# Strassen's scheme for half of the input projections of a differential attention layer (one core, fp32r)

## The reference, cut to what matters

```python
proj = u @ w_in                                   # (512, 2048) @ (2048, 8192)
q, k = split_heads(proj[..., :E], 16), split_heads(proj[..., E:2*E], 16)
v, z = split_heads(proj[..., 2*E:3*E], 8), proj[..., 3*E:4*E]
logits = q_blk @ k.T * scale + rel_bias           # masked above the diagonal
p = softmax(logits).reshape(B, 8, 2, Q_BLOCK, S)
a = p[:, :, 0] - lam * p[:, :, 1]
o = rms_norm(a @ v, subln_g) * (1.0 - lam_init)
y = (merge_blocks(o) * silu(z)) @ w_out           # (512, 2048) @ (2048, 2048)
h = layer_norm(ALPHA * x + y, ln_g, ln_b)
```

## Time and profile before

| | |
|---|---|
| median of 3 runs | 942.35 us |
| the profiled execution: its own time, its span | 942.39 us, 940.6 us |
| TensorE busy | 99% of the span, granted clock 1.00 |
| VectorE, ScalarE, GpSimd busy | 59%, 34%, 7% |
| HBM traffic | 121 GB/s over the span |
| one pair (1 to 7) | 94.2 us, 384 projection matmuls |

### The profile page before, as it was taken

The page is one execution under the profiler, slowest core; times in us unless marked ns, Lnnn a source line. Parts: engine busy times, 40 slices in busy tenths (PEclk is TensorE's granted clock), DMA queues, the critical chain, the costliest instruction groups (busy, mean ns, idle before and its releaser), DMA issues.

```text
span 940.6 us, 11611 instructions
## 1 busy us (share of the span) xinstructions
PE 934.3 (99%) x4202; PEld 777.6 (83%) x4202; DVE 550.5 (59%) x1131; ACT 318.1 (34%) x558; POOL 66.4 (7%) x140
## 2 busy tenths in 40 slices
PE   9999999999999999999999999999999999999997
PEld 8888888888888888888888888888888888888886
DVE  5546764766466646664666466646664797324466
ACT  4423333333333333333333333333333454122311
POOL 2200010001000100010001000100000000000033
PEclk9999999999999999999999999999999999999999
DMA  8732342223222322232224222422232223542423
GB/s 317 270 104 72 100 132 97 82 95 134 93 85 94 135 92 86 94 135 91 87 92 137 90 88 89 139 89 89 90 112 89 89 90 122 201 159 90 157 103 121
DMA packets 34087, 108.88 MB, mean 116 GB/s; under 512 B 4352, under 2 KB 6400, under 8 KB 33808
## 3 DMA queue, kind: packets, MB, share of 16 engines
q1 hardware_dynamic: 28320, 93.60, 29.5%
q0 software_dynamic: 2336, 9.48, 3.0%
q10 hardware_dynamic: 3408, 5.51, 1.7%
HBM read 104.34 MB, written 9.48 MB: 121 GB/s over the span
## 4 chain that ended last, share of the span: by engine, by line
PE 99%; DMA 0%; DVE 0%; issue 0%; ACT 0%; SPq 0%; DVEq 0%; ACTq 0%
PE proj L1003 79%; PE att L1003 20%; DMA w_raw<-w_in_tiles_dram 0%; DVE big L995 0%; DVE last_stats L981 0%; ACT bias L654 0%; SPq L322 0%; DVE w_split L851 0%; DVE mean_var L984 0%; DVEq L983 0%; ACTq L653 0%
## 5 line engine op out<-in xcount | busy, mean ns | idle before, releaser
L1003 PE MATMUL proj<-w_split,xg_split 128*128 128x512 f32 x1680 | 385.2, 389 | 0.0
L1003 PEld LDWEIGHTS proj<-w_split,xg_split 128*128 128x128 f32 x1680 | 314.8, 188 | 65.2
L1003 PE MATMUL proj<-xg_split,w_split 128*128 128x512 f32 x1536 | 353.0, 389 | 0.2 <-DVE w_split L851 0.2
L1003 PEld LDWEIGHTS proj<-xg_split,w_split 128*128 128x128 f32 x1536 | 287.5, 188 | 59.6 <-issue 0.5
L460 ACT ACTIVATE w_split<-w_raw 128x1024 fp32r<-128x1024 f32 x128 | 135.8, 1061 | 383.6 <-PE proj L1003 354.5
L675 DVE TENSOR_TENSOR w_split<-w_raw,w_split 128x1024 fp32r<-128x1024 f32 x128 | 155.5, 1224 | 175.6 <-ACT w_split L460 173.8
L749 DVE STREAM_TRANSPOSE scratch<-scratch 32x192 f32<-32x192 f32 (+2 forms) x384 | 141.8, 369 | 5.2
L1003 PE MATMUL att<-w_split,xg_split 128*128 128x512 f32 x432 | 99.9, 389 | 0.0
L1003 PEld LDWEIGHTS att<-w_split,xg_split 128*128 128x128 f32 x432 | 81.0, 188 | 16.8
L928 DVE TENSOR_TENSOR w_split<-w_raw,w_split 128x1024 fp32r<-128x1024 f32 x25 | 30.5, 1225 | 58.1 <-ACT w_split L619 58.0
L421 POOL TENSOR_SCALAR mean_sq<-sq_sum 128x1 f32<-128x1 f32 x32 | 10.3, 323 | 701.6 <-ACT scratch L511 700.3
(11 more groups left out here) (116 smaller groups left out, 428.1 us busy)
## 6 DMA issues: line engine op xcount, KB each, us to landing
w_raw<-w_in_tiles_dram SPq DMA_DIRECT2D x126, 512.0 KB, 3.3
w_raw<-w_out_tiles_dram SPq DMA_DIRECT2D x32, 512.0 KB, 3.3
bias_by_distance<-bias_lines POOLq DMA_DIRECT2D x8, 640.0 KB, 5.1
bias<-bias_by_distance POOLq DMA_DIRECT2D x8, 512.0 KB, 4.1
x_res<-in_x_dram ACTq DMA_DIRECT2D x4, 1024.0 KB, 6.2
big<-x_cols_dram SPq DMA_DIRECT2D x7, 512.0 KB, 9.1
out_dram<-big SPq DMA_DIRECT2D x10, 256.0 KB, 2.5
w_raw<-w_in_tiles_dram SPq DMA_DIRECT2D x4, 256.0 KB, 4.7
```

The source lines that it names most:

```text
L1003: return nc.tensor.matmul(dst, lhsT, rhs, start=start, stop=stop, skip_group_check=True)
```

## The change

For pairs 1 to 7, the first eight k-tiles of the q/k product and those of the v/z product are done by Strassen's scheme (in a form with few additions) on a 2 x 2 block split: seven block products of half size in place of eight. x is cut into k-tiles 0 to 3 and 4 to 7, and positions 0 to 255 and 256 to 511; the weights into the same k-tiles and two column blocks. The last eight k-tiles are multiplied as before. A pair now has 22 slots (`SLOTS`), two phases of 11 (`PHASE`): seven block products, then four plain quarters. Phase h = 0 is q and k, h = 1 is v and z. A block product has 24 matmuls of **256** moving columns.

- **x sums** (`x_sum`, `x_sum_lo`, `x_sum_hi`): four block sums of x, made and split once, during pair 0, into `x_sums`, which lies where `big` (raw x, later the output rows and `g`) was.
- **weight sums** (`w_sum`): four per phase on VectorE, each a TENSOR_TENSOR of 128x1024; the sums then go through the same splits as the raw blocks. There are 22 splits a pair in place of 16.
- **PSUM bookkeeping**: after product 1 ScalarE copies a result (`keep_copies`) and VectorE adds another to it (`keep_sums`); after product 3 ScalarE copies the corners (`keep_corners`) and VectorE adds both back into PSUM (`seed_corners`); then `seed_highs` writes the last regions. TensorE waits for `sum_kept` ahead of product 4, for `corner_seeded` ahead of product 5, for `high_seeded` ahead of product 6.
- **g goes through DRAM**: since `x_sums` holds `big`'s place, ScalarE stores each pair's gated output (`g_stored`, a DMA on its queue), and SP reloads seven of them in pair 7, once slot 17 is done. VectorE's first `combine` of a pair waits for `g_stored`.
- **order**: scores t = 0, 1 now come after slot 16 and t = 2, 3 after slot 18 of 22, `weigh_v` after slots 6 and 8, `turn_gated` in slot 10, ahead of `k_chunk`, `turn_a_early` in slot 20. All three transposes stay on VectorE and keep their number and size.

```diff
-                for j in range(QUARTERS):
-                    if j < VZ:
-                        quarter(p, j)
+                for j in range(SLOTS):
+                    if j % PHASE < 7:
+                        product(p, j)
+                    elif j < PHASE:
+                        plain_qk(p, j)
                     else:
-                        vz_part(p, j)
-                    late_inserts(p - 1, j)
-                    own_inserts(p, j)
+                        plain_vz(p, j)
+                    inserts(p, j)
...
+            def product(p, j):
+                h, r = j // PHASE, j % PHASE
+                pe.wait_ge(w_ready, slots_before(p) + j + 1)
...
+                for group in range(2):
+                    if opens and h == 0:
+                        bank = 2 * group + side
+                        pe.wait_ge(vz_moved, p * ST - ST + bank + 1)
...
+                    elif opens:
+                        pe.wait_ge(k_moved, 2 * p + group + 1)
+                    elif r == 4:
+                        pe.wait_ge(sum_kept, phases_before(p) + h + 1)
+                    elif r == 5:
+                        pe.wait_ge(corner_seeded, 2 * (phases_before(p) + h) + group + 1)
+                    elif r == 6:
+                        pe.wait_ge(high_seeded, 2 * (phases_before(p) + h) + group + 1)
...
+                    for kk in range(SK):
+                        first = opens and kk == 0
+                        if h == 0:
+                            mm(dst, w[0][:, kk, part], xs[0][:, kk], first, False)
+                            mm(dst, w[0][:, kk, part], xs[1][:, kk], False, False)
+                            last = mm(dst, w[1][:, kk, part], xs[0][:, kk], False, False)
...
+            def w_sum(p, h, n):
+                b11, b12, b22, b21 = (w_raw[:, i] for i in range(4))
+                if n == 1:
...
+                    op = nc.vector.tensor_tensor(b12, b12, b11, ALU.subtract)
+                elif n == 2:
...
+                    op = nc.vector.tensor_tensor(raw_fifth, b22, b12, ALU.subtract)
+                elif n == 3:
+                    op = nc.vector.tensor_tensor(b11, raw_fifth, b11, ALU.subtract)
+                else:
+                    op = nc.vector.tensor_tensor(raw_fifth, b21, raw_fifth, ALU.subtract)
+                op.then_inc(t_ready, 1)
...
+            def slot(p, j):
+                h, r = j // PHASE, j % PHASE
+                if j == PHASE:
                     k_chunk(p)
+                if 17 <= j < 20:
+                    logits_of(p, j - 17)
+                if j == 20:
                     combine(p, 2)
                     logits_of(p, 3)
                 split_lo_at(p, j)
+                if r == 0:
+                    w_sum(p, h, 4)
+                if r == 2:
+                    keep_sums(p, h)
+                if r == 3:
+                    seed_corners(p, h)
+                if r == 4:
+                    seed_highs(p, h)
+                late_steps(p - 1, j)
...
+                    if r == 8:
+                        w_sum(ahead, half, 1)
+                        w_sum(ahead, half, 2)
+                    if r == 9:
+                        w_sum(ahead, half, 3)
+                if j == 9:
                     q_chunk(p)
+                if j == 21:
+                    combine(p, 3)
+                if j == 20:
                     turn_a_early(p)
```

More of the change, by code:

```diff
@@ L417, in _ @@
                     spread_bias(p + 1)
+            load_bias(0)
+            for p in range(PAIRS):
+                if p + 1 < PAIRS:
+                    load_bias(p + 1)
                 for t in range(ST):
@@ new lines, in seed_corners @@
+            def seed_corners(p, h):
+                for group in range(2):
+                    n = 2 * (phases_before(p) + h) + group + 1
+                    dve.wait_ge(copy_kept, 3 * (phases_before(p) + h) + group + 2)
+                    low, corner = region(h, group, 1, 0), region(h, group, 1, 1)
+                    nc.vector.tensor_tensor(low, low, kept_sum[:, group], ALU.add).then_inc(low_seeded, 1)
+                    dve.wait_ge(low_seeded, n)
+                    nc.vector.tensor_tensor(corner, low, kept_copy[:, group], ALU.add).then_inc(corner_seeded, 1)
@@ L739, in combine @@
                 dve.wait_ge(mix_ready, n)
+                if t == 0 and not first_pair(p):
+                    dve.wait_ge(g_stored, 16 * p)
                 cols = slice(0, (t + 1) * P)
@@ L871, in _ @@
             for j in range(QUARTERS):
-                slot(0, j, False)
+                first_slot(j)
+                if j in X_SUMS_AT:
+                    for i in X_SUMS_AT[j]:
+                        x_sum(i)
                 if j in (1, 3, 5):
@@ new lines, in plain_vz @@
+            def plain_vz(p, j):
+                part = j - PHASE - 7
+                pe.wait_ge(w_ready, slots_before(p) + j + 1)
+                w = [w_split[:, SPLIT_OF[j], l].rearrange("p (k n) -> p k n", k=VK) for l in range(2)]
+                for s in range(ST):
+                    rows = slice(s * P, (s + 1) * P)
+                    dst = proj[:, s]
+                    for kk in range(VK):
+                        k = PLAIN_K + part * VK + kk
+                        x_hi, x_lo = xg_split[:, 0, k, rows], xg_split[:, 1, k, rows]
+                        mm(dst, x_hi, w[0][:, kk], False, False)
+                        mm(dst, x_hi, w[1][:, kk], False, False)
+                        last = mm(dst, x_lo, w[0][:, kk], False, k == KT - 1)
+                    if s == ST - 1:
+                        last.then_inc(quarter_done, 1)
+                    elif j == SLOTS - 1:
+                        last.then_inc(vz_done, 1)
```

604 lines of the change are left out of this document (450 added, 154 removed).

## The result

| | before | after |
|---|---|---|
| median | 942.4 us | 955.5 us (953.8 to 956.2, 4 runs) |
| profiled execution: time, span | 942.39, 940.6 us | 953.76, 951.5 us |
| TensorE, VectorE, ScalarE busy | 99%, 59%, 34% | 97%, 74%, 40% |
| mean granted clock | 1.00 | 0.993; 0.988 to 0.989 in the other executions |

The ratio is 1.0134 (95% interval 1.0117 to 1.0152): slower, by 13.1 us where I had forecast 4.6. It lies inside the range of 932 to 962.

What follows compares the result with a forecast made beforehand. TensorE's stream was taken to bound the kernel. From 942.4 us, 24.8 saved on TensorE and 29.2 of added waits gave 946.8, 947 us; the range was 932 to 962, the forecast's own 942 to 953.

Steps and rivals of the forecast that it cites:

- The sign: Whole kernel: slower than before, above 944.2 us, given a chance of 0.65.
- the chains on VectorE: VectorE's ordered work ahead of what TensorE needs: waits of 3.65 us a pair, 29.2 us in all.
- the saving on TensorE: Block products in pairs 1 to 7: 256-column matmuls at 0.119 us save 3.54 us a pair, 24.8 in seven.
- rival (E): Block products: weight loads bind in long runs at 0.188 us a matmul, 162 us more on TensorE, 1080 us; 3%.
- VectorE's load: VectorE's work per pair: up from 56.0 to 78.6 us of about 91, 86%.
- The end of a pair: From tile 2's scores to the first bank of v and z: TensorE waits 2.0 us.
- The start and the middle: TensorE waits 0.9 us ahead of product 4 and 0.7 us ahead of product 13 in a pair.
- The wait at product 15: Middle of a pair, after k moves, splits, a sum and keep_sums on VectorE: TensorE waits 0.1 us.
- Pair 1's at products 3 and 4: Edge from pair 0 to 1: the same 2.9 us of waiting, placed at products 3 and 4.
- The end of pair 7: Entrance of the output projection: splits of g and attention tiles stand ahead of the first bank; TensorE waits 3.6 us.
- rival (D): After the 7 waits of 2 to 3.6 us: granted clock falls, 2.86 us more each, 967 us; 5%.
- within: Whole kernel: time not told from no change, between 940.5 and 944.2 us; chance 0.13.

Runs made afterwards that it cites:

- e1_fill: The changed kernel with unused matmuls filling TensorE's waits, 8 ahead of each of pairs 1 to 7 and 14 ahead of the output projection: 951.8 us.
- e2_more: The changed kernel with two more 128x512 additions on VectorE ahead of turn_a_early in each of pairs 1 to 7: 969.0 us.
- e3_end: The changed kernel with two weight sums one slot earlier and turn_a_early ahead of the split of slot 20, pair 0 likewise: 931.6 us.
- e7_noturn: The changed kernel doing only 1 of 16 blocks of each transpose on VectorE, only the time being read: 922.4 us.
- e8_endkeep: e3_end with the copies and additions of keep_sums moved ahead of the split in slots 2 and 13: 927.0 us.
- e10_endmid: e3_end with half of turn_gated moved from slot 10 to behind the split of slot 12: 931.5 us.
- e6_all: The changed kernel with the moves of e3_end, e8_endkeep and e10_endmid, and one g split and both attention splits behind pair 7's first bank: 920.5 us.

## Why the prediction was wrong

The sign and the chains on VectorE were right; the clock was missing from the sum, and the saving on TensorE was put too high. Step by step:

- *The saving on TensorE.* Small matmuls start 0.120 us apart (mean 0.1198 of some 2,350 in the trace after); I had 0.119. The saving is 3.2 us a pair (94.20 less 91.01) in place of 3.54, 2.4 us less over seven pairs. The waits of a pair came to 3.55 (94.56 less 91.01) where I had 3.65, so the pair is 94.55 us where I had 94.3: 1.7 us over seven. The 0.188 of rival (E) did not occur: loads overlap in long runs as in short ones. In this trace the record of a load is 190 ns long and weight loads are busy 83 of 92 us, and still the spacing held at 0.120. The Trainium skill puts a load of 128 columns at 107 ns ("TensorE: Matmul & The Clock Gate", LDWEIGHTS); the records are longer than that, but the spacing shows no load that lacked cover behind 256 columns.
- *VectorE's load.* Forecast 78.6 us a pair, measured 76.9. The weight sums take 1.22 us and give way after 1.14, like the splits.
- *The end of a pair.* Forecast 2.0 us. Row: 1.8 and its 0.26, so 2.07. The chain runs as added up, from the split to the restart 11.56 us (465.70 to 477.26), where I had 11.6.
- *The start and the middle.* Forecast 0.9 and 0.7; measured 0.7 and 0.6 (0.43 and 0.34 in the rows, and 0.26 each). The wait at product 15 is 0.13 for 0.1. Pair 1's at products 3 and 4: 1.4 and 0.9 in the rows, 2.8 together with 0.26 each, for a forecast of 2.9.
- *The end of pair 7.* Forecast 3.6, measured 3.6 in the row, 3.7 by the starts of matmuls.
- **The step that failed: "In this trace it is 1.00 throughout, also right after a pause of 1.68 us", said of the granted clock, with which rival (D) got 5% and the sum nothing.** A pause of 1.7 us said nothing of pauses of 2 and 3.6 us. The clock fell after two of six waits of 2 us and at the last in the profiled execution; the others, whose mean clock is lower, spent more time at the lower level. In the profiled execution this is 0.8 us in each of two pairs and 2.4 at the entrance of the output projection (13 matmuls in 5.39 us, where they take 2.95 at full clock). That is 4 of the 6.5 us that the span is longer than forecast (10.9 against 4.4); the other parts are the 1.7 above and about 0.8 at the start and behind the last wait. The usual execution, with a mean clock of 0.988 to 0.989, takes another 1.6 to 2.4 us. e1_fill gives 3.2 to 3.7 of it back, net of fillers that cost about 2.3.
- *The price in (D)* was off too: 2.86 us for each of 7 waits. A fall behind a pair's start cost 0.8: 15 or 16 matmuls, not the 24 of a product, ran 0.213 us apart, 1.5 us more, and the wait at product 4, 0.7 us, went away.
- *A slip in the chances:* a sixth of the forecast's 50% is 0.08, not the 0.13 given to "within". It has no part in the time.

Over all traces: the waits of 2.0 us ahead of pairs 2 to 7 in the profile after were followed by a fall in two of six cases. Those of 3.3 us and more (seven in e2_more, the last one in the profile after) came with one every time. The waits of 1.9 us ahead of the output projection in e3_end, e7_noturn, e8_endkeep and e10_endmid came with none. That agrees with what I cited beside (D) from the Trainium skill, that long pauses bring the array back to half clock ("TensorE: Matmul & The Clock Gate", Loop structure matters more than you think). The trace of before could not show it, and I should have put a part of (D) into the sum, with seven such waits forecast.

What stays open: why two of six equal waits were followed by a fall and four were not, and a difference of up to 2.4 us between executions at the start (pair 1 begins between 95.5 and 97.9 us in the profiles, e1_fill's left out).

## What to carry to other kernels

Fewer columns on the engine that is the bound pay only as far as the helpers keep their order ahead of it: here 22 us of saving became 13 us of loss by the order of VectorE and by the clock that fell behind the waits it made. Moving a transpose and two sums brought back 24 of these 35 us, and the further moves of e6_all the rest. Add up the helper's list from the last event that it must wait for to the first signal that the bound engine needs, not its busy share, which was 74% of the span in the changed kernel and 77% in the fastest version, for the same 707 us of work. And where such a wait is as long as the ones here that were followed by the lower clock (2 us and more), add what that can cost.

## What the hardware showed unasked

- Adding 1.33 us to seven waits cost 1.9 us each, since the clock then fell at every one of them (mean 0.981).
- Matmuls of 256 fp32r columns, each with its own weight load, keep 0.120 us apart over whole block products, 0.227 at 512: against the 0.107 and 0.213 that 256 and 512 columns take at 2.4 GHz, about 0.013 us goes with each of either width.
